# The expert sublayer of a two-layer decoder: sixteen more tokens take U's activations by fetched rows, the U tiles multiply 368 tokens instead of 384

## The chip, the core and the metric

The kernel runs on one core of a Trainium2 chip. A core has a matrix engine (TensorE, PE in the profile), a vector engine (VectorE, DVE), an activation engine (ScalarE, ACT), a general engine (GpSimd, POOL) and SyncE (SP), which here only issues transfers; 16 DMA engines move data between HBM and the on-chip memory SBUF. TensorE writes to a second memory, PSUM. Each engine runs its own list of instructions in order; they meet through semaphores. The metric is the device time of one execution in microseconds, as the median of several runs.

## The reference, cut to what matters

Each of two layers has a mixer and then an expert sublayer, which the change is about:

```python
def peer_ffn(h, w_query, sub_keys1, sub_keys2, expert_u, expert_v):
    """PEER: 8 retrieval heads over N = n_keys^2 single-neuron experts."""
    ...
    expert = e1 * PEER_NKEYS + e2           # 8 heads x 16 experts for each token, of 16384
    gate = softmax(top_v)
    act = gelu(einsum("td,thkd->thk", xt, expert_u[et]), approximate=False) * gt
    return einsum("thk,thkd->td", act, expert_v[et])
```

There are 512 tokens of width 1024, and 128 picked experts for each token. All data is float32.

## The kernel before

Matrices stream from HBM as tiles of 128x1024 (512 KB). The kernel splits each tile into a high part (`w_hi`, by ScalarE, line 729) and a low part (`w_lo`, by GpSimd at line 630 or by VectorE at line 2133), and a product is the sum of three: high by high, high by low, low by high. Ring buffers hold four tiles.

The experts are worked in two ways. For the first 384 tokens (`DENSE_T`) they are **dense**: the kernel computes the activations of all 16384 experts, and multiplies them by a matrix of gates that is zero where an expert isn't picked. For the last 128 tokens (one on each partition) they are **fetched**: for each of 128 picks GpSimd issues a gather of one row of U for each token (line 648), and VectorE multiplies it by the token's h and sums (line 2167, a "dot"; h lies in PSUM as `h_rows`, the name `gbank` in the rows); later the same with rows of V.

A layer's expert sublayer runs in this order, after the scores (8 heads, two halves):

- **U tiles**, 128 of them, `u_tile`: 8 blocks of 128 of the width, three products each, 24 matrix products with 384 moving columns in a tile (lines 1212 to 1214). ScalarE takes the gelu (line 973) and writes it to HBM.
- Beside U tiles 0 to 25 VectorE ranks the scores and ends with `ex`, the picked experts and their gates (line 2113). Then TensorE turns `ex` (line 1546, three groups of four), and ScalarE and VectorE make `exT`, `gate_lo` and the first one-hot planes from it.
- From U tile 26 on (`U_EARLY`), gates are made beside the U tiles: for every four tokens (a quad) VectorE makes one-hot planes (`hot` and `plane`, lines 2142 and 2147), ScalarE their low parts (line 1010), TensorE multiplies them in two pairs (line 1560), ScalarE takes the high half of the sums (line 1020) and VectorE adds the low half (line 2156). A pair comes every 49/12 eighths of a tile, so nearly two in a tile. TensorE's pair p waits for the sums of pair p-3 and for the planes of its quad.
- `turn_h`, before U tile 27: TensorE turns the 128 fetched tokens' h into `h_rows`, 16 products with 128 columns (line 1533). From there on GpSimd and VectorE work through U's fetched rows, nine in eight tiles (`rows_of`), with four buffers: the fetch of row j+3 waits for dot j-1. GpSimd's order in a tile is: the low part of the tile two ahead, then the fetches.
- **V tiles**, 128 of them, 18 products with 512 columns each (line 1232), beside them the last 15 dots of U and the 128 rows of V.

Neither the V tiles nor the mixers are touched by the change.

Of the kernel before, what the change touches and what calls it, by code (L numbers as in the profile page):

```python
# [5 lines left out]
F32 = mybir.dt.float32  # L6
# [32 lines left out]
DENSE_C = DENSE_T // P  # L39
PICKS = PH * TOPK  # L40
# [43 lines left out]
U_DOTS = max(rows_of(n).stop for n in range(U_EARLY, NKEYS))  # L84
# [45 lines left out]
def evacuators():  # L130
# [8 lines left out]
          "exT": 5, "hot": QUADS, "one": QUADS, "one_lo": QUADS, "gate_lo": 1, "g_mm": PAIRS_OF_TOKENS, "g_hi": PAIRS_OF_TOKENS, "g_out": PAIRS_OF_TOKENS, "stored0": 16 * PIECES * ((STORED + 1) // 2), "stored1": 16 * PIECES * (STORED // 2), "picked": 2,  # L139
          "h_rows": 1, "u_row": 16 * PICKS // U_ROWS, "v_row": 16 * PICKS // V_ROWS, "dotted": PICKS, "z_gel": 2,  # L140
# [81 lines left out]
def build(nc, stream, x_t, c, ada, ada_b, gains, gate_b, conv_w, mnorm, keys, qk_norm, u0, v0, u1, v1, out_t):  # L222
# [174 lines left out]
    u_rows = sb("u_rows", [P, U_ROWS, D])  # L397
    assert place[0] <= limit - 4 * DENSE_T * 4 - (limit % 64)
# [86 lines left out]
    def _(sp_):  # L485
# [75 lines left out]

        done = RING
        for layer in range(2):
# [10 lines left out]
            loads(done, DENSE[layer] + FIRST_UNIT_AT + UNIT_LEAD)  # L574
# [16 lines left out]
    def _(pool):  # L591
# [52 lines left out]
        def u_fetch(layer, j):  # L644

            past = counted(layer)
            wait(pool, S("dotted"), past["dotted"] + j - U_ROWS + 1)
            pool.indirect_dma_start(u_rows[:, j % U_ROWS, :], None, (u0, u1)[layer],  # L648
                                    bass.IndirectOffsetOnAxis(ap=row_of[:, j:j + 1], axis=0)
                                    ).then_inc(S(f"u_row{j % U_ROWS}"), 16)  # L650
# [9 lines left out]
        def peer(layer):  # L660

            past = counted(layer)
            for n in range(U_EARLY, U_GATED):
                if n == U_EARLY:
# [6 lines left out]
            for j in range(rows_of(U_GATED).start + U_ROWS - 1, min(PICKS, U_DOTS + U_ROWS - 1)):  # L671
                u_fetch(layer, j)
            pool.wait_ge(tile_done, DENSE[layer] + NKEYS)
            for j in range(PICKS):
                v_fetch(layer, j)
                dotted = dot_beside(j - V_ROWS)
                if dotted is not None and dotted + U_ROWS - 1 < PICKS:
                    u_fetch(layer, dotted + U_ROWS - 1)
# [42 lines left out]
    def _(act):  # L721
# [219 lines left out]
        def peer(layer):  # L941
# [23 lines left out]
            def u_tile(n, off=0, pairs=()):  # L965
# [7 lines left out]
                act.activation(gel[:, s, :], bank[t % 2][:, 0:DENSE_T], ACT.Gelu).then_inc(emptied_sem["a"], 1)  # L973
# [30 lines left out]
            def low_planes(q):  # L1004

                if q == 0:
                    act.wait_ge(S("gate_lo"), past["gate_lo"] + 1)
                act.wait_ge(S("hot"), past["hot"] + q + 1)
# [30 lines left out]
            for n in range(U_EARLY, NKEYS):  # L1039
# [1347 lines left out]
```

## Time and profile before

| | us |
|---|---|
| median of 3 runs | 3041.66 (3039.47 to 3042.04) |
| the profiled execution, its own time | 3040.28 |
| its span, first to last instruction | 3038.6 |
| TensorE busy | 2991.3 (98%) |
| VectorE busy | 2526.6 (83%) |
| GpSimd busy | 1589.9 (52%) |
| ScalarE busy | 1530.0 (50%) |
| moved by DMA | 846.18 MB, 278 GB/s on average |

The page's picture of the span in 40 slices shows where the stages lie: the U tiles of layer 0 run from 388 to 972 us and the V tiles to 1494 us; layer 1 has the same from 1921 and 2506 us. TensorE's busy digit is 9 in all slices but the first. The DMA digit is 4 to 6 in the tiles 0 to 25 of U, then 9. A share of busy time says little by itself: a matrix product's record is longer (0.33 us) than the distance to the next one, since they overlap. The pace is read from the distance of starts.

### The profile page before, as it was taken

Reading aid. Unit: us, or ns where it says so; the run is one execution under the profiler, and the core shown is the slowest. Engines: PE = TensorE matmul, PEld = TensorE weight load, DVE = VectorE, ACT = ScalarE, POOL = GpSimd, SP = SyncE. Lnnn points to the kernel's source line nnn. Section 1 sums busy time; section 2 is a strip of 40 time slices with the busy share of each in tenths; the row PEclk is TensorE's granted clock in tenths of the full one; section 3 lists DMA queues with packets and bytes.
Section 4 is the critical chain, followed back from the end, with each engine's and each line's share of the span. In section 5 each row is a group of like instructions: output and inputs, shape, how many; then the busy total and the mean of one; then the engine's idle time right before and its main releaser. Section 6 shows DMA issues by size and latency. Waiting matters only on the chain.

```text
span 3038.6 us, 45145 instructions
## 1 busy us (share of the span) xinstructions
PE 2991.3 (98%) x15480; PEld 2663.9 (88%) x15480; DVE 2526.6 (83%) x5006; ACT 1530.0 (50%) x2833; POOL 1589.9 (52%) x974
## 2 busy tenths in 40 slices
PE   6999999999999999999999999999999999999999
PEld 4888899999999888888787788999999998888887
DVE  7987998888887999998745949988888888888887
ACT  4345335776775333343464743347777763333332
POOL 3434357777776555452255634577777765322221
PEclk9999999999999999999999999999999999999999
DMA  6732246899999999999546422458999999999996
GB/s 256 248 110 104 85 156 220 323 325 345 344 325 360 395 391 393 390 391 373 190 164 211 115 66 84 140 196 310 333 326 355 334 357 374 384 373 366 346 351 229
DMA packets 320607, 846.18 MB, mean 278 GB/s; under 512 B 28208, under 2 KB 149056, under 8 KB 320400
## 3 DMA queue, kind: packets, MB, share of 16 engines
q1 hardware_dynamic: 189952, 437.83, 41.1%
q0 software_dynamic: 74000, 268.81, 24.0%
q10 hardware_dynamic: 56448, 136.86, 12.1%
q8 instruction: 119, 1.95, 0.3%
q14 instruction: 88, 0.72, 0.1%
HBM read 735.91 MB, written 94.90 MB: 273 GB/s over the span
## 4 chain that ended last, share of the span: by engine, by line
PE 90%; DVE 6%; ACT 2%; DMA 1%; issue 1%; ACTq 0%; DVEq 0%; SPq 0%; POOL 0%; POOLq 0%
PE banks L1232 23%; PE banks L1212 12%; PE banks L1214 12%; PE banks L1213 12%; PE gbank L1232 11%; PE banks L1192 4%; PE banks L1193 4%; PE banks L1194 4%; PE gbank L1560 2%; PE banks L1560 1%; PE gbank L1513 1%; PE banks L1291 1%; DMA ada_mid<-ada_dram 1%; DVE sp_lo L2311 1%; ACT sp L1115 1%
## 5 line engine op out<-in xcount | busy, mean ns | idle before, releaser
L630 POOL TENSOR_TENSOR w_lo<-raw,w_hi 128x1024 fp32r<-128x1024 f32 x351 | 901.9, 2573 | 537.4 <-ACT w_hi L729 534.4
L729 ACT ACTIVATE w_hi<-raw 128x1024 fp32r<-128x1024 f32 x613 | 646.5, 1055 | 601.0 <-PE banks L1232 373.4
L1212 PE MATMUL banks<-h_hi,w_hi 128*128 128x384 f32 x2048 | 687.0, 335 | 0.0
L1214 PE MATMUL banks<-h_hi,w_lo 128*128 128x384 f32 x2048 | 684.4, 334 | 0.0
L1213 PE MATMUL banks<-h_lo,w_hi 128*128 128x384 f32 x2048 | 684.3, 334 | 0.0
L656 POOL DMA_INDIRECT v_rows<-v_dram,row_of x256 | 356.1, 1391 | 619.6 <-DVE fetched L2182 603.6
L1212 PEld LDWEIGHTS banks<-h_hi,w_hi 128*128 128x128 f32 x2048 | 384.5, 188 | 0.0
L1213 PEld LDWEIGHTS banks<-h_lo,w_hi 128*128 128x128 f32 x2048 | 384.5, 188 | 0.0
L1214 PEld LDWEIGHTS banks<-h_hi,w_lo 128*128 128x128 f32 x2048 | 384.4, 188 | 0.0
L648 POOL DMA_INDIRECT u_rows<-u_dram,row_of x256 | 253.9, 992 | 204.9 <-DVE z L2167 169.9
L2182 DVE SCALAR_TENSOR_TENSOR fetched<-v_rows,share,fetched 128x1024 f32<-128x1024 f32 x254 | 326.5, 1285 | 3.6 <-DMA v_rows<-v_dram,row_of 3.2
L1232 PE MATMUL banks<-w_hi,a_hi 128*128 128x512 f32 x1024 | 315.3, 389 | 0.0
L1232 PE MATMUL banks<-w_lo,a_hi 128*128 128x512 f32 x1024 | 315.3, 389 | 0.0
L1232 PE MATMUL banks<-w_hi,a_lo 128*128 128x512 f32 x1024 | 315.3, 389 | 0.0
L2133 DVE TENSOR_TENSOR w_lo<-raw,w_hi 128x1024 fp32r<-128x1024 f32 x258 | 314.2, 1218 | 0.0
L2167 DVE CUSTOM_DVE_ANT_0 u_rows<-u_rows,gbank 128x1024 f32<-128x1024 f32 x256 | 308.9, 1214 | 0.0
L1010 ACT ACTIVATE plane<-hot,gate_lo 128x128 fp32r<-128x128 f32 x768 | 246.3, 391 | 83.6 <-ACT gel L973 66.6
L1192 PE MATMUL banks<-h_hi,w_hi 128*128 128x512 f32 x672 | 267.2, 398 | 2.2 <-POOL w_lo L630 2.2
L1194 PE MATMUL banks<-h_hi,w_lo 128*128 128x512 f32 x672 | 262.3, 390 | 0.0
L1193 PE MATMUL banks<-h_lo,w_hi 128*128 128x512 f32 x672 | 262.2, 390 | 0.0
L973 ACT ACTIVATE gel<-banks 128x384 f32<-128x384 f32 x256 | 125.7, 491 | 246.1 <-PE banks L1214 240.6
L2142 DVE TENSOR_TENSOR hot<-banks,exT 128x1024 fp32r<-128x1024 f32 x192 | 234.3, 1220 | 17.1 <-PE gbank L1560 10.5
(377 smaller groups left out, 5049.0 us busy)
## 6 DMA issues: line engine op xcount, KB each, us to landing
raw<-stream_dram SPq DMA_DIRECT2D x613, 512.0 KB, 6.5
gel_dram<-gel ACTq DMA_DIRECT2D x248, 192.0 KB, 4.2
gin<-gel_dram SPq DMA_DIRECT2D x62, 768.0 KB, 10.9
g_dram<-stage ACTq DMA_DIRECT2D x56, 768.0 KB, 9.4
gates<-g_dram SPq DMA_DIRECT2D x64, 672.0 KB, 7.3
ada_w<-ada_dram ACTq DMA_DIRECT2D x36, 512.0 KB, 7.4
ada_mid<-ada_dram ACTq DMA_DIRECT2D x24, 512.0 KB, 4.4
ada_first<-ada_dram SPq DMA_DIRECT2D x8, 1024.0 KB, 17.7
```

The costliest lines, as they stand in the source:

```text
L630: pool.tensor_tensor(w_lo[:, s, :], raw[:, s, :], w_hi[:, s, :].bitcast(F32), ALU.subtract).then_inc(split_lo, 1)
L656: pool.indirect_dma_start(v_rows[:, j % V_ROWS, :], None, (v0, v1)[layer], bass.IndirectOffsetOnAxis(ap=row_of[:, j:j + 1], axis=0)).then_ ...
L729: act.activation(w_hi[:, s, :], raw[:, s, :], ACT.Copy).then_inc(split_hi, 1)
L1192: pe.matmul(out, wh, hi(k), start=(k == 0), stop=False)
L1193: pe.matmul(out, wh, lo(k), start=False, stop=False)
L1194: mm = pe.matmul(out, wl, hi(k), start=False, stop=(k == DC - 1))
L1212: pe.matmul(out, wh, h_hi[:, k, 0:DENSE_T], start=(k == 0), stop=False)
L1213: pe.matmul(out, wh, h_lo[:, k, 0:DENSE_T], start=False, stop=False)
L1214: mm = pe.matmul(out, wl, h_hi[:, k, 0:DENSE_T], start=False, stop=(k == DC - 1))
L1232: mm = pe.matmul(sums[c][half][:], a, w[:, half * SEQ:(half + 1) * SEQ], start=(v == 0 and a is ah and w is hi), stop=(v == NKEYS - 1 and ...
L2133: dve.tensor_tensor(w_lo[:, s, :], raw[:, s, :], w_hi[:, s, :].bitcast(F32), ALU.subtract).then_inc(split_lo, 1)
L2182: add = dve.scalar_tensor_tensor(out=fetched[:], in0=row, scalar=share[:, j:j + 1], in1=fetched[:], op0=ALU.mult, op1=ALU.add)
```

## The change

In both layers, the last 16 of the 384 dense tokens no longer go through the U tiles: a U tile's products have 368 moving columns instead of 384. What those 16 tokens need is 16 x 128 = 2048 dots of a U row with their h. They are done as 16 more fetched rows in the same loop, rows 28 to 43 of now 144, an eighth of the picks of one token on each partition: partition 16 q + i holds the h of token i and, for the 16 rows, its picks 16 q to 16 q + 15. For that

- VectorE also computes the expert numbers of the last dense block (a memset and two small instructions after line 2123's place), and SyncE copies them and the gates, 16x16 pieces, to `row_extra` and `share_extra`: 16 small transfers, two ahead of each of 8 tile loads;
- TensorE turns the 16 tokens' h first (`turn_extra`, 16 products with a stationary block of 16 columns, before U tile 27), ScalarE copies it from PSUM to SBUF (`h_extra`, 16x1024), and SyncE copies it seven times down the partitions, one copy ahead of each of seven tile loads. `turn_h` is now before U tile 28 and waits for ScalarE's copy, since both use `h_rows`;
- the 16 extra dots read `h_extra`, which lies in SBUF, where the others read `h_rows` in PSUM;
- rows go at 23 in 18 tiles instead of 9 in 8, so that the V tiles have the same 15 dots as before;
- later ScalarE takes the gelu of the extra dots, VectorE multiplies by the gates and transposes blocks, SyncE gathers them back by 8 small transfers, and the result stands in the dense gates in the place of the 16 tokens' gates (`gate_extra_hi`, `gate_lo`). In the dense activations those tokens get the constant 1 (a copy of `ones` into `gel` once a layer), so V's products are as before;
- GpSimd takes the low part of tile 28 ahead of its first three fetches instead of behind them.

```diff
-    return range(min(PICKS, 9 * (n - ROWS_FROM) // 8), min(PICKS, 9 * (n - ROWS_FROM + 1) // 8))
+    return range(min(U_SUMS, 23 * (n - ROWS_FROM) // 18), min(U_SUMS, 23 * (n - ROWS_FROM + 1) // 18))
+U_SUMS = EXTRA + PICKS
+EXTRA_FROM = 28
...
+        def spread_extra(layer, q):
+            if q == 0:
+                sp_.wait_ge(S("picked"), counted(layer)["picked"] + 3)
...
+        def copy_extra(layer, q):
+            if q == 1:
+                sp_.wait_ge(S("extra_by_act"), counted(layer)["extra_by_act"] + H_ROWS_COPIED)
+            sp_.dma_start(h_extra[picks_of(q), :], h_extra[0:EXTRA, :]).then_inc(S("extra_moved"), 16)
...
             for n in range(U_EARLY, U_GATED):
+                low(DENSE[layer] + n + LOW_AHEAD)
                 if n == U_EARLY:
                     pool.wait_ge(S("picked"), past["picked"] + 2)
                     for j in range(U_ROWS - 1):
                         u_fetch(layer, j)
-                low(DENSE[layer] + n + LOW_AHEAD)
...
+                if n == ROWS_FROM:
+                    act.wait_ge(S("h_rows"), past["h_rows"] + 1)
+                    act.activation(h_extra[0:EXTRA, :], h_rows[0:EXTRA, :], ACT.Copy).then_inc(S("extra_by_act"), 1)
                 u_tile(n, pairs=[p for p in range(PAIRS_OF_TOKENS) if pair_step(p) // DC == n])
...
-                pe.matmul(out, wh, h_hi[:, k, 0:DENSE_T], start=(k == 0), stop=False)
-                pe.matmul(out, wh, h_lo[:, k, 0:DENSE_T], start=False, stop=False)
-                mm = pe.matmul(out, wl, h_hi[:, k, 0:DENSE_T], start=False, stop=(k == DC - 1))
+                pe.matmul(out, wh, h_hi[:, k, 0:DENSE_U], start=(k == 0), stop=False)
+                pe.matmul(out, wh, h_lo[:, k, 0:DENSE_U], start=False, stop=False)
+                mm = pe.matmul(out, wl, h_hi[:, k, 0:DENSE_U], start=False, stop=(k == DC - 1))
...
+            def turn_extra():
+                pe.wait_ge(S("exT"), past["exT"] + 2)
+                for k in range(DC):
+                    out = h_rows[0:EXTRA, k * P:(k + 1) * P]
+                    for n, h in enumerate((h_hi, h_lo)):
+                        last = pe.matmul(out, h[:, k, DENSE_U:DENSE_T], ident_r[:], start=(n == 0), stop=(n == 1))
+                last.then_inc(S("h_rows"), 1)
             def turn_h():
-                pe.wait_ge(S("exT"), past["exT"] + 2)
+                pe.wait_ge(S("extra_by_act"), past["extra_by_act"] + H_ROWS_COPIED)
...
                 if n == ROWS_FROM:
+                    turn_extra()
+                if n == ROWS_FROM + 1:
                     turn_h()
...
                 if j == 0:
-                    dve.wait_ge(S("h_rows"), past["h_rows"] + 1)
-                dve.tensor_tensor_reduce(row, row, h_rows, 1.0, 0.0, ALU.mult, ALU.add, z[:, j:j + 1]
-                                         ).then_inc(S("dotted"), 1)
+                    dve.wait_ge(S("h_rows"), past["h_rows"] + 2)
+                if j == EXTRA_FROM:
+                    dve.wait_ge(S("extra_moved"), past["extra_moved"] + EXTRA_COPIED)
+                e, m = j - EXTRA_FROM, main_row(j)
+                h, to = (h_extra[:], z_extra[:, e:e + 1]) if is_extra(j) else (h_rows, z[:, m:m + 1])
+                dve.tensor_tensor_reduce(row, row, h, 1.0, 0.0, ALU.mult, ALU.add, to).then_inc(S("dotted"), 1)
```

Two places show how the lists of instructions change. The first is ScalarE between `exT` and the gelu of U tile 27, in layer 0. In the kernel before (`plane` are the low one-hot planes of the first two quads, `w_hi` the high part of a tile three ahead, `gel` the gelu of tile 26):

```order
L1010 ACTIVATE plane<-hot,gate_lo 128x128 x8
L729 ACTIVATE w_hi<-raw 128x1024
L973 ACTIVATE gel<-banks 128x384
L976 DMA gel_dram<-gel 128x384
L729 ACTIVATE w_hi<-raw 128x1024
L1020 ACTIVATE stage<-banks 128x128x2
L973 ACTIVATE gel<-banks 128x384
```

In the changed kernel:

```order
L1098 ACTIVATE plane<-hot,gate_lo 128x128 x8
L812 ACTIVATE w_hi<-raw 128x1024
L1059 ACTIVATE gel<-banks 128x368
L1062 DMA gel_dram<-gel 128x384
L1130 ACTIVATE h_extra<-gbank 16x1024
L812 ACTIVATE w_hi<-raw 128x1024
L1108 ACTIVATE stage<-banks 128x128x2
L1059 ACTIVATE gel<-banks 128x368
```

The copy to `h_extra` stands behind the gelu of tile 26 and its store, and TensorE's `turn_h` waits for it.

The second is VectorE around U tile 49. In the kernel before (the pair `L2167 ISA` is one dot; its operand `gbank` is `h_rows` in PSUM):

```order
L2142 TENSOR_TENSOR hot<-banks,exT 128x1024
L2147 TENSOR_TENSOR plane<-hot,banks 128x4x128
L2156 TENSOR_TENSOR stage<-stage,gbank 128x128x2
L2167 ISA u_rows,z<-u_rows,gbank 128x1024
L2167 ISA z 128x1
```

In the changed kernel:

```order
L2257 TENSOR_TENSOR hot<-banks,exT 128x1024
L2262 TENSOR_TENSOR plane<-hot,banks 128x4x128
L2271 TENSOR_TENSOR stage<-stage,gbank 128x128x2 x2
L2286 ISA u_rows,z_extra<-u_rows,h_extra 128x1024
L2286 ISA z_extra 128x1
```

The dot's second operand is now in SBUF, as its first is, for 16 dots in a row; every other instruction of VectorE in this stage still reads one of its operands from PSUM.

## Rows read from the trace of the kernel before

**Rows 1.** The page: the chain that ended last, by engine.

```profile
PE 90%; DVE 6%; ACT 2%; DMA 1%; issue 1%; ACTq 0%; DVEq 0%; SPq 0%; POOL 0%; POOLq 0%
```

**Rows 2.** Timeline of TensorE, U tiles (start us, us, engine, line, names, shape).

```profile
440.29 0.33 PE L1212 MATMUL banks<-h_hi,w_hi 128*128 128x384 f32 x1
...
444.44 0.33 PE L1212 MATMUL banks<-h_hi,w_hi 128*128 128x384 f32 x1
```

**Rows 3.** The chain in order of time (start us, us, engine, line, count).

```profile
974.01 2.72 PE banks L1232 x12
978.09 2.72 PE banks L1232 x12
...
1809.49 2.88 PE gbank L1291 x24
```

**Rows 4.** Timelines of VectorE, then TensorE, before U tile 26 of layer 0.

```profile
493.41 1.67 DVE L2113 TENSOR_TENSOR ex<-ex,red 128x512 f32<-128x512 f32 x1
...
499.31 0.56 DVE L2125 TENSOR_TENSOR gate_lo<-gbank,hot 128x384 f32<-128x384 f32 x1 [3.51 <-ACT banks L1002]
...
495.93 1.47 PE L1546 MATMUL gbank<-ident,ex 128*128 128x128 f32 x12
```

**Rows 5.** Timeline of TensorE: turn_h, U tile 27, first pairs of tokens.

```profile
501.41 0.22 PE L1533 MATMUL gbank<-ident_r,h_hi 128*128 128x128 f32 x1
...
503.03 0.28 PE L1533 MATMUL gbank<-ident_r,h_lo 128*128 128x128 f32 x1
...
507.60 0.40 PE L1560 MATMUL gbank<-plane,hot 128*128 128x256 f32 x2
```

**Rows 6.** Timeline of ScalarE, the same stretch; then its splits of a tile (page).

```profile
505.64 0.34 ACTq L976 DMA_DIRECT2D gel_dram<-gel  x1
...
L729 ACT ACTIVATE w_hi<-raw 128x1024 fp32r<-128x1024 f32 x613 | 646.5, 1055 | 601.0 <-PE banks L1232 373.4
```

**Rows 7.** TensorE's waits (us in total, times, longest us).

```profile
PE banks L1270 <- ACT h_hi L790: 11.8, 2, 8.8
...
PE gbank L1600 <- ACT av L1104: 4.0, 2, 3.6
PE banks L1275 <- DVE h_lo L1801: 3.4, 2, 1.7
```

**Rows 8.** Stretches: busy time of the engines, TensorE's granted clock, DMA share, GB/s.

```profile
48.00:56.00 8.00, 5.59 (x23) 4.31 (x24) 5.39 (x10) 2.06 (x4) 0.00 (x0) 1.00 0.36 132
1508.80:1515.60 6.80, 5.82 (x14) 4.59 (x15) 6.80 (x12) 6.68 (x12) 0.00 (x0) 0.50 0.00 1
1655.55:1658.95 3.40, 3.40 (x14) 2.90 (x15) 2.52 (x5) 3.27 (x6) 2.99 (x2) 0.50 0.01 2
```

**Rows 9.** Line 1560, matrix products of a pair: idle time before it.

```profile
  issue: 3.5, 12
  DVE plane L2147: 1.2, 4
```

**Rows 10.** Stretches, as rows 8: 96 U tiles, then part of the V tiles.

```profile
515.00:960.00 445.00, 444.98 (x2675) 442.94 (x2673) 365.03 (x588) 318.09 (x754) 331.00 (x202) 1.00 0.93 336
1000.00:1400.00 400.00, 400.00 (x1767) 331.24 (x1766) 368.11 (x557) 150.97 (x199) 197.66 (x111) 1.00 1.04 391
```

**Rows 11.** Groups of instructions in 515 to 960 us (busy, mean ns, idle before).

```profile
L630 POOL TENSOR_TENSOR w_lo<-raw,w_hi 128x1024 fp32r<-128x1024 f32 x95 | 229.5, 2416 | 22.4 <-ACT w_hi L729 21.0
...
L2167 DVE CUSTOM_DVE_ANT_0 u_rows<-u_rows,gbank 128x1024 f32<-128x1024 f32 x108 | 130.2, 1214 | 0.0
```

**Rows 12.** VectorE's waits from 500 to 962 us, the longest.

```profile
DVE stage L2156 <- ACT stage L1020: 71.9, 94, 3.8
```

**Rows 13.** VectorE's groups, shapes apart, over the whole span.

```profile
L2133 DVE TENSOR_TENSOR w_lo<-raw,w_hi 128x1024 fp32r<-128x1024 f32 x258 | 314.2, 1218 | 0.0
...
L2106 DVE TENSOR_TENSOR pick<-pick 128x1024 f32<-128x1024 f32 x4 | 13.2, 3308 | 0.1
```

**Rows 14.** DMA issues in 515 to 960 us (count, median us to landing).

```profile
u_rows<-u_dram,row_of POOLq DMA_INDIRECT x107, 7.0
```

More of the change, by code:

```diff
@@ L39 @@
 DENSE_C = DENSE_T // P
+EXTRA = 16
+DENSE_U = DENSE_T - EXTRA
+GROUPS_OF_PICKS = P // EXTRA
+EXTRA_ROWS = slice(DENSE_U % P, DENSE_U % P + EXTRA)
 PICKS = PH * TOPK
@@ L397, in build @@
     u_rows = sb("u_rows", [P, U_ROWS, D])
+    h_extra = sb("h_extra", [P, D])
+    row_extra = sb("row_extra", [P, EXTRA], U32)
+    share_at = place[0]
+    share_extra = sb("share_extra", [P, EXTRA])
+    z_extra = sb("z_extra", [P, 2 * EXTRA])
+    gate_extra = z_extra[:, 0:EXTRA]
+    turned_extra = sb("turned_extra", [P, 2 * EXTRA])
+    u_end = place[0]
+    place[0] = share_at
+    gate_extra_hi = sb("gate_extra_hi", [P, EXTRA], F32R)
+    place[0] = u_end
     assert place[0] <= limit - 4 * DENSE_T * 4 - (limit % 64)
@@ L573, in _ @@
                 done = OUT1 + LEAD + RING
-            loads(done, DENSE[layer] + FIRST_UNIT_AT + UNIT_LEAD)
+            done_to = DENSE[layer] + U_EARLY + RING + 2
+            loads(done, done_to)
+            for q in range(GROUPS_OF_PICKS):
+                spread_extra(layer, q)
+                load_after(done_to + q)
+            done_to += GROUPS_OF_PICKS
+            for q in range(1, GROUPS_OF_PICKS):
+                copy_extra(layer, q)
+                load_after(done_to + q - 1)
+            loads(done_to + GROUPS_OF_PICKS - 1, DENSE[layer] + EXTRA_LOAD)
+            done_to = DENSE[layer] + EXTRA_LOAD
+            for q in range(GROUPS_OF_PICKS):
+                gather_extra(layer, q)
+                load_after(done_to + q)
+            loads(done_to + GROUPS_OF_PICKS, DENSE[layer] + FIRST_UNIT_AT + UNIT_LEAD)
             for s in range(2):
@@ L667, in peer @@
                         u_fetch(layer, j)
-                low(DENSE[layer] + n + LOW_AHEAD)
                 for j in rows_of(n):
                     u_fetch(layer, j + U_ROWS - 1)
-            for j in range(rows_of(U_GATED).start + U_ROWS - 1, min(PICKS, U_DOTS + U_ROWS - 1)):
+            for j in range(rows_of(U_GATED).start + U_ROWS - 1, min(U_SUMS, EXTRA + U_DOTS + U_ROWS - 1)):
                 u_fetch(layer, j)
@@ L677, in peer @@
                 if dotted is not None and dotted + U_ROWS - 1 < PICKS:
-                    u_fetch(layer, dotted + U_ROWS - 1)
+                    u_fetch(layer, EXTRA + dotted + U_ROWS - 1)
         lows(RING, DENSE0 + U_EARLY + LOW_AHEAD)
@@ L1053, in gelu_rows @@
                 own = slice(n * Z_HALF, Z_HALF if n == 0 else PICKS)
[L1054 removed]
+                act.wait_ge(S("dotted"), past["dotted"] + EXTRA + own.stop)
                 act.activation(z[:, own], z[:, own], ACT.Gelu).then_inc(S("z_gel"), 1)
@@ L1205, in u_tile @@
             pe.wait_ge(emptied_sem["a"], emptied("a", t - 2) + off)
-            out = bank[t % 2][:, 0:DENSE_T]
+            out = bank[t % 2][:, 0:DENSE_U]
             for k in range(DC):
@@ L2123, in peer @@
             dve.tensor_copy(share[:], last_ex[2]).then_inc(S("picked"), 1)
+            extra_ex = [ex[:, n, DENSE_C - 1].rearrange("p h k -> p (h k)") for n in range(2)]
+            dve.memset(z_extra[:, EXTRA:], 0.0)
+            link(dve.scalar_tensor_tensor(out=z[:], in0=extra_ex[0], scalar=float(NKEYS), in1=extra_ex[1],
+                                          op0=ALU.mult, op1=ALU.add))
+            dve.tensor_copy(expert[:].bitcast(U32), z[:]).then_inc(S("picked"), 1)
             dve.wait_ge(S("exT"), past["exT"] + 5)
@@ L2231, in peer @@
                 if dot_beside(v) is not None:
-                    dot(dot_beside(v))
+                    dot(EXTRA + dot_beside(v))
                 add_row(v)
```

64 lines of the change are left out of this document (57 added, 7 removed).

## The prediction

> **What bounds the kernel now.** I read the chain that ended last first: nine tenths of it are TensorE [rows 1], so time goes where TensorE's own list gets shorter, and stays where the next engine is late. Then the pace of its products, from the distance of starts. In the U tiles 24 products take 444.44 - 440.29 = 4.15 us, 173 ns each, for 384 columns [rows 2]. A V tile's 18 products of 512 columns come every 4.08 us, 227 ns each, and 24 products of 256 columns take 2.88 us, 120 ns each [rows 3]. The three lie on one line: 0.417 ns for a column, and 13 ns beside. So columns are the bound in the U tiles, and 16 fewer are worth 16 x 0.417 = 6.7 ns a product. That weight loads set the pace, so that narrower products win nothing, is excluded by the 120 ns.
>
> Then, for each engine that hands something to TensorE, how late it already is: before tile 26 [rows 4], at tile 27 [rows 5, 6], at the pairs [rows 9], and over the 96 tiles beside the gates [rows 10 to 12].
>
> **What the columns bring.** 24 x 6.7 ns = 0.16 us a tile, 128 tiles, two layers: -41.0 us.
>
> **Where the first part of it goes: tile 26.** TensorE starts to turn `ex` at 495.93 [rows 4], 12 products at 0.11 us (1.47 us less the overlap of the last); the last four start at 496.8. They need the last `ex`, which VectorE ends at 493.41 + 1.67 = 495.08 [rows 4], only 1.7 us earlier. VectorE isn't held by TensorE there, so its time stays, while TensorE comes 26 x 0.16 = 4.16 us earlier, at 492.65. It waits until about 495.2: 2.55 us lost in a layer, +5.1 us for both. VectorE's own additions behind that (a memset of 16 columns, a sum and a cast of 128) are each shorter than the 0.56 us of 384 columns behind them, which sits idle for 3.51 us on ScalarE [rows 4]; of that cover 1.6 goes with the earlier turns and 1.9 is left for under 1.7, so they are hidden. GpSimd's low part of tile 28 moves 2.4 us of work [rows 11] ahead of three fetches; these land late by as much, but the first dot now waits longer anyway, for `turn_h`.
>
> **Tile 27 and 28.** `turn_extra` is 16 more products of 128 columns. The same count in `turn_h` takes 503.03 - 501.41 and one more, 1.75 us [rows 5]; a stationary block of 16 columns instead of 128 may be quicker to load, and 128 columns can't pass in less than 53 ns each: 0.9 to 1.8 us; I take 1.1. Then `turn_h` waits for the copy to `h_extra`. ScalarE issues tile 26's store at 505.64 for 0.34 us [rows 6]; its work there hangs on `exT`, so it comes 1.6 us earlier, and ends at 504.4. The copy has 1024 columns, as a split of a tile, 1.06 us [rows 6]: done at 505.5. TensorE: tile 26 from 495.55, 4.0 us, turn_extra 1.1, tile 27 with a pair 4.24: there at 504.9, waits 0.65, then `turn_h`. With 1.8 instead of 1.1 it comes when the copy is done, so either value gives the same. Cost 1.75 us a layer, +3.5. After this the pair that now starts at 507.60 [rows 5] starts at 507.4: of the first 28 tiles' 4.5 us, 0.2 is left.
>
> **The clock.** A wait of 2.55 us is new. The longest waits in this trace are 3.6 us and (11.8 less 8.8) 3.0 us [rows 7], and behind each the granted clock is 0.50 (1.2 GHz) for 3.4 and 6.8 us [rows 8]; two waits of 1.7 us [rows 7] lie in a stretch at 1.00 (2.4 GHz) [rows 8]. Mine lies between. 3.4 us at half rate cost 1.7 us, of which 0.65 would have been waited for the copy: 1.05 a layer. Bounds: none, or 6.8 us twice, 5.5 us. I take one fall in one of the two layers, +1.0.
>
> **The pairs.** TensorE stood idle before a pair 16 times, 4.7 us in all [rows 9]: where an odd pair opens a tile, the next pair needs planes that ScalarE starts only behind the gelu. There the half tile before gets no shorter: 16 x 0.08 = +1.3.
>
> **VectorE and the shared way.** VectorE is busy 365.03 of 445 us, 3.81 of 4.64 us a tile [rows 10] (the 4.64: 24 products of 173 ns, and 1.96 pairs of two products at 120 ns); 23/18 rows instead of 9/8 add 0.153 x 1.214 us [rows 11], so 4.0 of 4.48. Its idle time is mostly a wait for ScalarE, 71.9 us [rows 12], which a late VectorE doesn't have. But the 16 extra dots have both operands in SBUF. Such an instruction and GpSimd's low part shut each other out here: an addition of 1024 columns takes 3308 ns where GpSimd splits, a subtraction of the same shape 1218 ns where it doesn't [rows 13], against 2416 ns for an undisturbed low part [rows 11], so about one low part is waited for. The Trainium skill has this as a rule (SBUF — State Buffer, "Who interferes with whom"): a VectorE instruction with two SBUF inputs contends with a GpSimd instruction that reads SBUF, and the later one waits for the whole of the other. It speaks against this change, and the trace agrees, by the rows just named. GpSimd is at a low part for 2.42 of 4.48 us. A dot can wait 0 to 2.42 us, so 0 to 38.7 us a layer. If a dot waited for a low part, the next one is due just when the next low part starts or ends, so VectorE settles a fixed 1 to 2 us behind and TensorE, which needs the sums only three pairs later, about 7 us, sees little. I take 0.5 us a layer, +1.0.
>
> **Rows that land late.** A fetched row lands 7.0 us after its issue (median) [rows 14]. Four rows pass between a buffer's turns: 4 x 4.64 / 1.125 = 16.5 us now, 4 x 4.48 / 1.278 = 14.0 then, less dot, issue and a low part, about 4.6: 9.4 us. The 16 rows are 8.4 MB more, and the rate goes from 336 GB/s to some 365, under the 391 of the V tiles [rows 10]. In bursts some rows will be late. 0 to 2 us a layer, taken as 0.5, +1.0. SyncE's small transfers stand between tile loads and take nothing that TensorE sees; the two waits on it are for things long done when the loads ahead have been let go.
>
> **Sum.** -41.0 + 5.1 + 3.5 + 1.3 + 1.0 + 1.0 + 1.0 = -28.1. Against the profiled execution's 3040.28: 3012.2. The median of the runs is 1.4 above that: 3013.6.
>
> **Rivals.**
>
> *Dots queue behind low parts, and it shows* (no change): each extra dot waits half a low part, 1.2 us. 16 x 1.2 = 19.4 us a layer; the 12.5 tiles they lie in have 0.48 us to spare each, 6 us, so 13.4 is left, 26.8 in both, instead of the 1.0 above: 3039.4. For it: the rows on the lock. Against: the slack of three pairs, and that waits for ScalarE vanish when VectorE is late. Cases between this and the forecast are likelier than the full one.
>
> *The same lock, and slower than before*: each extra dot waits for a whole low part, 2.42 us: 38.7 - 6 = 32.7 a layer, 65.4 in both: 3078. From 1.3 us of wait a dot on, all slack used, the change loses. For it: in the first tiles beside gates the low part starts just ahead of the dot, tile after tile. Against: VectorE, once late, starts behind the low part.
>
> *The DMA engines are the bound*: their share is 0.93 in this stretch [rows 10]. If 336 GB/s were all that this mix can carry, 8.4 MB would take 25 us in a layer, and the stage grows by that instead of shrinking by 16: 3041.66 + 50 = 3092. Against: 391 GB/s a little later, and that VectorE's list has no wait for a row among its longest.
>
> **How the numbers follow.** The forecast, 3008 to 3019: 0.6. Between it and the first rival, 3019 to 3035: 0.26. The first rival in full, 3035 to 3048: 0.06. Slower, by the lock 0.05, by the DMA engines 0.03. The lower end has none of clock, lock and late rows: 3010.6, and some for error in the pace: 3008. The upper end adds the bounds 4.5 (clock), 8 (lock, half seen) and 2 (rows): 3028. A measurement of this kernel can tell 0.2%, 6 us, from no change: faster 0.86, same 0.06, slower 0.08.
>
> **What would show it.** U tiles 4.0 us apart before tile 26 (right: the pace). TensorE waiting some 2.5 us on VectorE at the turns of `ex`, about 0.65 us on ScalarE before `turn_h`. V tiles of layer 0 starting 14 to 15 us earlier than 972. Extra dots of up to 3.6 us in VectorE's rows with the low parts beside them (the lock); TensorE's waits on line 2156's sums or on low parts in the tiles 49 to 61 would say that it shows. Wrong it would be if U tiles stay at 4.16 us, if the dots wait for rows tile after tile, or if VectorE's ranking itself moves with the faster tiles.

## The result, and the profile after

The changed kernel takes 3017.55 us in the median (3015.15 to 3018.09, 4 runs) against 3041.5 before (3039.47 to 3042.04, 4 runs): a ratio of 0.9921, with a 95% interval of 0.9906 to 0.9937. It is 24 us faster. The forecast was 3013.6, 28 us faster, and the range 3008 to 3028. The profiled execution took 3017.35 us, its span is 3015.6.

The pace first. TensorE's timeline among the early U tiles (start us, us, engine, line, operation; line 1309 is line 1212 of before). Eight products of this line, so 24 in all, are one tile:

```profile
447.81 0.33 PE L1309 MATMUL banks<-h_hi,w_hi 128*128 128x368 f32 x1
...
451.81 0.33 PE L1309 MATMUL banks<-h_hi,w_hi 128*128 128x368 f32 x1
```

4.00 us a tile against 4.15 in [rows 2]. Next the place of [rows 4], TensorE's first product of U and the turns of `ex`:

```profile
388.21 0.41 PE L1309 MATMUL banks<-h_hi,w_hi 128*128 128x368 f32 x1
...
492.31 1.47 PE L1652 MATMUL gbank<-ident,ex 128*128 128x128 f32 x12
```

and VectorE's last step of the ranking (line 2221 for 2113) and its subtraction for `gate_lo`, which has no idle time ahead of it any more:

```profile
490.74 1.68 DVE L2221 TENSOR_TENSOR ex<-ex,red 128x512 f32<-128x512 f32 x1
...
495.69 0.56 DVE L2238 TENSOR_TENSOR gate_lo<-gbank,hot 128x384 f32<-128x384 f32 x1
```

The ranking ends at 492.42, 104.2 us behind U's first product. Before it was 495.08 - 387.65 = 107.4. The last four of the turns' products, which need it, start at 493.18: of the 1.7 us that it was ahead of them, 0.8 is left, though TensorE came earlier, and the wait that I had put at 2.55 us does not exist. Then the turn of the 16 rows, and ScalarE's copy of them, the places of [rows 5, 6]:

```profile
497.64 0.22 PE L1630 MATMUL gbank<-ident_r,h_hi 128*16 128x128 f32 x1
...
498.53 0.22 PE L1630 MATMUL gbank<-ident_r,h_lo 128*16 128x128 f32 x1
```

```profile
502.40 1.01 ACT L1130 ACTIVATE h_extra<-gbank 16x1024 f32<-16x1024 f32 x1 [0.42 <-ACT gel L1059]
```

Sixteen products come 0.06 us apart, and tile 27 starts at 498.59: about 1.0 us. What TensorE waits for in the whole span, as in [rows 7] (us in total, times, longest):

```profile
PE banks L1367 <- ACT h_hi L873: 11.8, 2, 8.8
...
PE gbank L1666 <- DVE stage L2271: 6.2, 2, 3.1
PE gbank L1708 <- ACT av L1201: 4.5, 2, 3.7
...
PE gbank L1329 <- DVE w_lo L2246: 1.3, 3, 0.7
...
PE gbank L1639 <- ACT h_extra L1130: 0.8, 2, 0.4
```

The wait for the copy is there, 0.4 us in each layer. The largest new row is another: 3.1 us, twice, for line 2271, VectorE's addition to `stage`, ahead of a pair of tokens. It stands at the very end of U, in both layers. TensorE's timeline there, and two stretches with the clock (columns as [rows 8]):

```profile
941.88 0.32 PE L1311 MATMUL banks<-h_hi,w_lo 128*128 128x368 f32 x1
945.29 0.47 PE L1666 MATMUL gbank<-plane,hot 128*128 128x256 f32 x2 [3.09 <-DVE stage L2271]
```

```profile
942.00:946.00 4.00, 0.91 (x7) 0.74 (x6) 1.28 (x3) 2.17 (x5) 1.51 (x1) 1.00 1.02 409
946.04:949.45 3.41, 3.41 (x13) 3.41 (x12) 2.85 (x7) 2.69 (x5) 1.91 (x3) 0.50 0.75 262
```

VectorE had waited for ScalarE, and ScalarE (first row below, its waits from 880 to 950 us) for a tile of the stream, 7.1 us. The chain that ended last goes through that tile's transfer (second row). Behind the wait the granted clock is 0.50 for 3.41 us: 13 products pass instead of 20, 1.7 us more.

```profile
ACT w_hi L812 <- DMA raw<-stream_dram: 7.5, 2, 7.1
```

```profile
924.17 19.17 DMA raw<-stream_dram
```

That transfer stands on SyncE's queue behind the loads of V's first two units. The DMA issues of 515 to 960 us (KB each, median us to landing) show them slower than in the kernel before, where the same three rows were 5.9, 11.3 and 16.3; below, the stretches of [rows 10]:

```profile
raw<-stream_dram SPq DMA_DIRECT2D x98, 512.0 KB, 6.6
...
gates<-g_dram SPq DMA_DIRECT2D x2, 672.0 KB, 14.2
gin<-gel_dram SPq DMA_DIRECT2D x1, 768.0 KB, 19.5
```

```profile
515.00:940.00 425.00, 424.00 (x2636) 421.22 (x2635) 383.12 (x611) 307.52 (x744) 350.09 (x214) 1.00 0.97 361
1000.00:1400.00 400.00, 398.66 (x1755) 328.81 (x1754) 364.33 (x553) 152.07 (x200) 209.69 (x110) 1.00 1.03 386
```

361 GB/s are the some 365 of the working, with a share of 0.97. Last, the dots (VectorE's groups, whole span, shapes apart) and a wait that the kernel before does not have, VectorE's for rows from 500 to 962 us:

```profile
L2286 DVE CUSTOM_DVE_ANT_0 u_rows<-u_rows,gbank 128x1024 f32<-128x1024 f32 x256 | 307.4, 1213 | 14.6 <-DMA u_rows<-u_dram,row_of 13.3 <-PE gbank L1639 1.0
L2286 DVE CUSTOM_DVE_ANT_0 u_rows<-u_rows,h_extra 128x1024 f32<-128x1024 f32 x32 | 52.1, 1642 | 0.8 <-DMA u_rows<-u_dram,row_extra 0.8
```

```profile
DVE u_rows L2286 <- DMA u_rows<-u_dram,row_of: 6.0, 5, 3.1
```

Where the 23.0 us between the two profiled spans lie, from the starts of the tiles in both traces (U counted from its first product to V's first): U got shorter by 12.4 us in layer 0 and 12.2 in layer 1; V is longer by 2.5 us in layer 0 and as long in layer 1 (522.1); the parts between and around are 0.9 us shorter.

### The profile page after: what moved, and what is told of

The parts are those of the page before. It is cut to its first block, busy times and chain, and to the rows that moved or that the text cites. A ratio compares the mean times of both kernels' runs of the same rounds, so it can differ in the third digit from the quotient of the medians.

```text
span 3015.6 us, 45245 instructions
## 1 busy us (share of the span) xinstructions
PE 2957.6 (98%) x15512; PEld 2624.1 (87%) x15512; DVE 2571.4 (85%) x5084; ACT 1521.9 (50%) x2841; POOL 1680.1 (56%) x1006
## 4 chain that ended last, share of the span: by engine, by line
PE 56%; DVE 23%; DMA 11%; issue 4%; ACT 4%; POOL 1%; SPq 0%; ACTq 0%; DVEq 0%; POOLq 0%
PE banks L1329 16%; PE gbank L1329 8%; DMA raw<-stream_dram 8%; PE banks L1309 6%; PE banks L1310 6%; PE banks L1311 6%; PE banks L1289 3%; PE banks L1291 3%; PE banks L1290 3%; DVE u_rows L2286 2%; DVE hot L2257 2%; DVE pick L2214 2%; DVE w_lo L2246 1%; PE gbank L1666 1%; DVE pick L2209 1%
## 5 line engine op out<-in xcount | busy, mean ns | idle before, releaser
L739 POOL DMA_INDIRECT v_rows<-v_dram,row_of x256 | 392.0, 1531 | 576.0 <-DVE fetched L2300 561.7
L1309 PE MATMUL banks<-h_hi,w_hi 128*128 128x368 f32 x2048 | 676.4, 330 | 0.0
L1310 PE MATMUL banks<-h_lo,w_hi 128*128 128x368 f32 x2048 | 674.0, 329 | 0.0
L1311 PE MATMUL banks<-h_hi,w_lo 128*128 128x368 f32 x2048 | 673.9, 329 | 0.0
L1329 PEld LDWEIGHTS banks<-w_lo,a_hi 128*128 128x128 f32 x1024 | 192.2, 188 | 40.0
```

The source lines that it names most:

```text
L739: pool.indirect_dma_start(v_rows[:, j % V_ROWS, :], None, (v0, v1)[layer], bass.IndirectOffsetOnAxis(ap=row_of[:, j:j + 1], axis=0)).then_ ...
L1309: pe.matmul(out, wh, h_hi[:, k, 0:DENSE_U], start=(k == 0), stop=False)
L1310: pe.matmul(out, wh, h_lo[:, k, 0:DENSE_U], start=False, stop=False)
L1311: mm = pe.matmul(out, wl, h_hi[:, k, 0:DENSE_U], start=False, stop=(k == DC - 1))
L1329: mm = pe.matmul(sums[c][half][:], a, w[:, half * SEQ:(half + 1) * SEQ], start=(v == 0 and a is ah and w is hi), stop=(v == NKEYS - 1 and ...
```

## The experiments

Each is set against runs of the kernel before on the same chip. Their median was 3040.5 us beside most of them, against 3041.5 beside the changed kernel, so medians of two batches can differ by 1 us for nothing. A trace is of one run: with full width it is the slowest of seven, with the dots, the early turn and both moves the fastest of four.

**The second unit's loads behind the stream.** The edit in SyncE's program:

```
-            for u in range(2):
-                load_unit(layer, u)
+            load_unit(layer, 0)
             for t in range(DENSE[layer] + FIRST_UNIT_AT + UNIT_LEAD, v0_ + NKEYS):
+                if t == v0_:
+                    load_unit(layer, 1)
```

> The changed kernel with one move on SyncE's queue: the loads of the second unit of V (its gates) are issued behind the last two raw tiles of the stream instead of ahead of them; the first unit's loads stay where they are. In the changed kernel TensorE stands for 3.1 us twice before the last tiles of U (in each layer; ScalarE had waited 7.1 us for a stream tile then) and the granted clock is 0.50 for 3.41 us behind it; I put this at about 4.8 us per layer. Theory (the last stream tiles of U land late because the units' loads are ahead of them in the queue): the waits of ScalarE and of TensorE at tiles 124 and 125 go, the clock stays at 1.00 there, and the time falls by 6 to 10 us, to about 3009. Rival (the DMA engines are full there whatever the order): the 3.1 us remain or only move to V's first tile, and the time is within 2 us of the changed kernel, 3016 to 3019.

The second unit's loads are `gates` and `gin`, 1.44 of the 2.1 MB that stood ahead of those tiles.

Measured: 3008.52 us (3006.08 to 3012.17), ratio 0.9901, 0.9884 to 0.9918. The stretch that was at a stand, and TensorE's waits from 480 to 950 us:

```profile
942.00:946.00 4.00, 4.00 (x26) 4.00 (x25) 2.83 (x6) 0.89 (x2) 2.41 (x3) 1.00 1.05 410
```

```profile
PE banks L1667 <- DVE stage L2272: 1.1, 1, 1.1
PE banks L1310 <- POOL w_lo L710: 0.5, 1, 0.5
PE gbank L1640 <- ACT h_extra L1131: 0.4, 1, 0.4
```

26 products where there were 7, at the same 410 GB/s, no stand and no fall of the clock in either layer. U is 3.2 and 5.0 us shorter than in the changed kernel; 1.4 us of layer 0's part went again at tile 61, behind a low part of GpSimd that came late (the 0.5 above), and at tile 82, where VectorE had waited 2.5 us for a late row (the 1.1). So the order on the queue makes the wait, and not only the full DMA engines. The time fell by 9 us against the changed kernel by the medians, which come from two batches; the two intervals of the ratio overlap, so the size rests on the traces, the mechanism on the row that went.

**The columns alone.** The kernel before with one constant changed in three products and the gelu. It leaves out the activations of the last 16 dense tokens, and copies a constant into their place once a layer:

```
-                pe.matmul(out, wh, h_hi[:, k, 0:DENSE_T], start=(k == 0), stop=False)
+                pe.matmul(out, wh, h_hi[:, k, 0:DENSE_U], start=(k == 0), stop=False)
```

> The kernel before with U's products and the Gelu 368 columns wide, and nothing else of the change: the activations of the last 16 dense tokens are left out (a constant stands in their place), no rows are added for them, nothing is copied or turned for them. It shows the columns alone. The early tiles should take 4.00 us against 4.16. What it tells apart. (a) The end of U: if the faster tiles alone make the stream late there, TensorE waits about 3 us at tiles 124 and 125 in this kernel too, and the time is about 3013; if it takes the added rows as well, the wait is not there and the time is about 3003 (3017.5 less 3.5 for the turns and their wait, less about 1 for the late rows, less 9.6 for the end of U). (b) The ranking: my prediction held that its end stands at 107.4 us from the first tile of U, so that tile 26 waits for some 2.5 us per layer; the rival that the changed kernel suggests is that this end moves by some us with the phase in which VectorE's and GpSimd's steps meet (it stood at 104.2 us there). If the end stands at 107.4 here, the tiles' pace does not move it and the changed code behind it did; if it stands at 103 to 106, the phase does.

Measured: 3000.12 us (2998.77 to 3000.35), ratio 0.9869, 0.9852 to 0.9885: 40.4 us less, of the sum's 41.0, and 3 below the lower of my two figures. V's tiles start 20.1 us earlier behind U's start in both layers. At the end of U ScalarE waits up to 2.3 us for a tile of the stream, but TensorE doesn't stand, so the faster tiles alone do not make its wait. And the ranking, with not one instruction of it changed, ends at 489.63 + 1.68 = 491.31, 104.2 us behind U's first product, as in the changed kernel. Answer to (b): the change's code did not move it, the pace did. What it ends with is a low part of GpSimd (second row, which ends at 490.76, 0.55 us ahead; third row, the same place in the kernel before, which ends 0.55 us ahead of 495.08):

```profile
489.63 1.68 DVE L2118 TENSOR_TENSOR ex<-ex,red 128x512 f32<-128x512 f32 x1
487.89 2.87 POOL L632 TENSOR_TENSOR w_lo<-raw,w_hi 128x1024 fp32r<-128x1024 f32 x1
491.67 2.86 POOL L630 TENSOR_TENSOR w_lo<-raw,w_hi 128x1024 fp32r<-128x1024 f32 x1
```

**All additions at the old width.** The reverse: the changed kernel with `DENSE_T` in those products.

> The changed kernel with U's products as wide as before, 384 columns (the last 16 dense tokens are then computed twice, the fetched way still gives the result): all that the change adds, without what it takes away. By the prediction's sums the additions on TensorE's path are 3.5 us for the turns and the wait for the copy, 1.3 at the pair waits and 1 for the late rows, 5.8 in all, so 3046 or so against 3040.3 of the kernel before. Theory (the end of U waits because the faster tiles meet an almost full DMA): at 4.16 and 4.64 us per tile the wait at tiles 124 and 125 is gone or under 1 us, and the time is 3044 to 3048. Rival (the denser rows alone make the stream late): the 3.1 us and the clock's fall remain, and the time is 3052 to 3056. If the extra dots cost more than they seem to (their lock on GpSimd's low parts), this shows too: each further 0.1 us per tile of the late stage is 18 us.

Measured: 3047.96 us (3043.76 to 3051.77, 7 runs), ratio 1.0025, 1.0014 to 1.0037. The additions cost 7.5 us at the old width and some 17 at the new one (3017.55 less 3000.12, of two batches). In the profiled execution (3051.77, the slowest) the turns cost 1.4 us a layer and the late rows nothing up to tile 124. The end of U is between the two expectations: TensorE waits there in both layers, 1.1 and 2.7 us, and the clock falls behind the longer one.

```profile
PE gbank L1666 <- DVE stage L2271: 3.7, 2, 2.7
```

So in these traces the narrow tiles alone make no wait, the added rows alone 3.7 us, and both 6.2. The ranking ends at 107.4 us here, though the changed code is all there.

**Dots without the second operand in SBUF.**

```
-                h, to = (h_extra[:], z_extra[:, e:e + 1]) if is_extra(j) ...
+                h, to = (h_rows, z_extra[:, e:e + 1]) if is_extra(j) ...
```

> The changed kernel with the added dots reading the common rows of h in PSUM, as the others do, instead of the copy of the 16 tokens' rows in SBUF: the U activations of the last 16 dense tokens are then made with other tokens' h and are wrong, everything else is as it is. Without two operands in SBUF the added dots should no longer hold each other up with GpSimd: in the changed kernel they take 1.85 us in the median (1.21 the least), and GpSimd's fetches with added rows 1.76 (0.95 the least). Theory (that wait is hidden: TensorE is never late by it): the added dots take 1.21, the fetches 0.95, and the time stays within 3 us of the changed kernel, 3015 to 3019, since the end of U waits for the stream as before. Rival (my prediction's: the lock costs TensorE 0.26 to 0.54 us per tile over the late stage): 3017.5 less 8 or more, under 3010.

Measured: 3015.49 us (3012.99 to 3018.66), ratio 0.9922, 0.9905 to 0.9938. The dots and GpSimd's fetches from 600 to 655 us (ns min, median, max), first of the changed kernel, then of this one:

```profile
L2286 DVE CUSTOM_DVE_ANT_0 u_rows<-u_rows,h_extra x14: 1215/1849/2100, 606.0 to 654.1; 128x1024 f32<-128x1024 f32 x14
L731 POOL DMA_INDIRECT u_rows<-u_dram,row_extra x14: 932/1757/1821, 602.7 to 653.2; - x14
```

```profile
L2286 DVE CUSTOM_DVE_ANT_0 u_rows<-u_rows,gbank x16: 1212/1214/1217, 601.0 to 652.4; 128x1024 f32<-128x1024 f32 x16
L731 POOL DMA_INDIRECT u_rows<-u_dram,row_extra x14: 934/950/952, 602.5 to 649.0; - x14
```

The lock is real and goes with the operand: 0.64 us on a dot, 0.81 on a fetch. Who waits for whom is seen in the changed kernel's timelines (VectorE, then GpSimd):

```profile
613.79 2.10 DVE L2286 CUSTOM_DVE_ANT_0 u_rows<-u_rows,h_extra 128x1024 f32<-128x1024 f32 x1
612.37 2.42 POOL L709 TENSOR_TENSOR w_lo<-raw,w_hi 128x1024 fp32r<-128x1024 f32 x1
614.95 1.76 POOL L731 DMA_INDIRECT u_rows<-u_dram,row_extra  x1 [0.16 <-issue]
```

The dot starts inside a low part and ends 1.1 us behind the low part's end (614.79); it waited for the low part's rest, and the fetch, issued behind the low part, for the dot. The dots of 1.21 us that meet a fetch already under way are not held.

The edit bought no time that the runs can tell. By the traces TensorE is 1.1 to 1.4 us further at tile 124 than in the changed kernel, so late rows and lock together cost about 2.5 us, both layers summed; the small losses at tiles 61 to 82 are gone. This kernel's V stage in layer 0 is 4.0 us longer than before, against 2.5.

**The 16 rows' turn one step earlier.** `turn_extra` ahead of U tile 24, the copy behind the gelu of that tile, `turn_h` back ahead of tile 27 (PE shown; ScalarE's copy moves with it):

```
+            turn_extra()
             for n in range(4 + (U_EARLY - 4) // 4 * 4, U_EARLY):
                 u_tile(t0 + n)
+            pe.wait_ge(S("extra_by_act"), past["extra_by_act"] + H_ROWS_COPIED)
...
                 if n == ROWS_FROM:
-                    turn_extra()
-                if n == ROWS_FROM + 1:
                     turn_h()
```

> The changed kernel with the turn of the 16 tokens' rows one step earlier: it stands ahead of U tile 24, ScalarE copies the rows behind its Gelu of tile 24, and the common turn of h stands where it did in the kernel before, ahead of tile 27, with the same wait for the ranking. In the changed kernel TensorE stands about 0.7 us in each layer behind the turn, waiting for ScalarE's copy, whose Gelu and stage come first. Theory: this wait goes, ScalarE's copy of 1.01 us costs nothing on TensorE's path, and 1.4 us are saved in both layers, 3016.1; the end of U then waits as before or some tenths longer, since the stream is no earlier: 3016 to 3017.5. Rival (ScalarE is late by its copy in that stage, and the tile behind waits for its emptied bank or for its w_hi): the 0.7 us come back at tiles 25 to 27, no gain or a loss of up to 2 us.

Measured: 3018.83 us (3013.4 to 3021.8), ratio 0.9935, 0.9918 to 0.9952: no gain. Up to tile 28 it did what it should: the wait for the copy is gone and, from U's first product, TensorE is 0.7 us earlier than in the changed kernel in both layers (0.69; the 0.85 of the next expectation is too high). In layer 1 the end of U took it back, as the row of TensorE's wait there shows (6.2 before this edit); in layer 0 it was gone before, with 1.6 us lost at tiles 60 and 61, where a low part of GpSimd came late behind a fetch that had waited for a dot:

```profile
PE gbank L1668 <- DVE stage L2271: 8.4, 2, 5.1
```

**Both moves.** 

> The changed kernel with both moves: the 16 tokens' turn and ScalarE's copy one step earlier, and the second unit's loads behind the last stream tiles. Alone, the second gave 3008.5 with no wait at the end of U; the first gave 0.85 us per layer ahead of tile 28, and lost it again at the end of U, where the waits grew to 3.3 and 5.1 us. Theory (what the early turn saves is given back only because the stream is late there): with the stream early the 0.85 us stay in both layers, 3008.5 less 1.7, 3006.8 (3004 to 3009). Rival (the early turn costs at tiles 60 to 62, where the run of it alone lost 1.3 us in the first layer): 3008 to 3010.

Measured: 3009.92 us (3003.23 to 3010.57), ratio 0.9901, 0.9884 to 0.9917. The profiled run is the fastest, 3003.23, with its 0.7 us kept up to tile 28 in both layers and no stand at the end of U; the other three are not faster than the loads' order alone. The early turn is therefore not shown to bring anything. Nor did I find out why these runs lie in two places, 7 us apart.

**Other widths: 376, 352, 356 and 372.** The first three are the columns-alone kernel with another constant, with one run each; the last is the changed kernel with the later loads and four columns more in U's products.

> The kernel before with U's products 376 columns wide (the activations of the last 8 dense tokens left out, a constant in their place), a tile of 4.08 us instead of 4.16. The ranking of the routes has no idle time and the same instructions at every width; its end stands at 107.4 us from the first tile of U at 384 columns and at 104.2 at 368, the same to 0.03 us in both layers and in kernels with and without the added rows. Theory (the phase of VectorE's steps against GpSimd's decides, and every step outside of the meetings has the same length): the end here is anywhere from 102 to 109 us and need not lie between the two. Rival (a faster pace makes the ranking end sooner, in proportion): 105.8, and 101 at 352 columns. The time should be 3040.5 less 0.08 x 256, 3020, within 3.

> As the run at 376 columns, with U's products 352 columns wide (the activations of the last 32 dense tokens left out), a tile of 3.84 us. Phase theory: the ranking's end stands anywhere from 102 to 109 us from U's first tile; it then comes about 0 to 7 us behind tile 26, which stands at 101.2, and tile 26 waits as my prediction had it for the changed kernel. Rival (in proportion to the pace): 101, and no wait. Time by the columns alone 3040.5 less 82, 2958.5; with the wait in both layers up to 10 more, and more if the stream's DMA or ScalarE becomes the bound at this pace.

> The kernel before with U's products 356 columns wide (the activations of the last 28 dense tokens left out, a constant in their place). At 384, 376, 368 and 352 columns a U tile of 24 products took 4.16, 4.16, 4.00 and 3.84 us: the 376 cost what 384 do. Theory (a product's time goes in steps of 16 columns): 356 cost what 368 do, 4.00 us per tile, the ranking's end stands at 104.2 us, and the time is about that of the run at 368 columns, 3000. Rivals: steps of 8 columns from a multiple of 32 (360: 3.92 us per tile, 2984 or so); time by the column, with 376 a special case (3.87 us per tile, 2973 or so, with up to 6 us of waits for the ranking).

> The changed kernel with the second unit's loads behind the last stream tiles, as in the run that gave 3008.5, and U's products 372 columns wide instead of 368 (four of the 16 tokens are then computed in the dense way too; the fetched way still gives the result). Early U tiles of 24 products took 4.16 us at 384 and at 376 columns, 4.00 at 368, and 3.84 at 356 and (late in the stage, 3.87 early) at 352: 173.3, 166.7 and 160.0 ns a product, at the clock of 2.4 GHz 416, 400 and 384 cycles. All five fit one rule: the columns and 25 to 28 cycles beside them, rounded up to a multiple of 16 cycles. By this rule 372 columns cost 400 cycles: 4.00 us per tile, and the time is that of the run with 368, 3008.5, within 3 us. Rival (the steps lie at multiples of 16 columns, with 356 a special case): 4.16 us per tile, and 0.16 x 256 = 41 us more, near 3045. The time also measures the gain by the loads' order a second time.

Measured: 3039.88, 2967.0, 2962.55, and 3024.3 (3022.82 to 3027.54; ratio 0.9947, 0.993 to 0.9963). How many products TensorE has in the same 80 us of early U tiles: 464 at 384 columns, 482 at 368, and at 376, 372, 356 and 352 columns, one row each (stretch, its length, busy time and count, clock, DMA share, GB/s):

```profile
400.00:480.00 80.00, 80.00 (x464) 1.00 0.54 173
```

```profile
400.00:480.00 80.00, 80.00 (x473) 1.00 0.52 175
```

```profile
400.00:480.00 80.00, 80.00 (x502) 1.00 0.54 180
```

```profile
400.00:480.00 80.00, 80.00 (x499) 1.00 0.55 179
```

By the tiles' starts, for 384, 376, 372, 368, 356 and 352, that is 173.3, 173.3, 170.0, 166.7, 160.0 and 161.1 ns a product. Eight columns less than 384 brought nothing at all; 356 cost less than 352 in these early tiles, and the same in the later ones (520 products from 600 to 680 us in both). My expectation of 3020 for 376 was wrong, as was each rule that I wrote down for the next run: the steps of 16 columns fell with 356, the rounding to 16 cycles with 372, where neither it nor its rival came out. I have no rule for these times. The forecast's straight line through 256, 384 and 512 columns held for 368 because 368 happens to lie on it: at 376 it gives 170.0, and 173.3 was measured.

The last run measured the loads' order again, in another way: at 4.08 us a tile, no wait at the end of U in either layer.

**The ranking, moved by hand.** The kernel before, with one step that no one waits for done three times, or six:

```
+            for _ in range(2):
+                link(dve.memset(fifteen[:], TOPK - 1))
             dve.memset(fifteen[:], TOPK - 1)
```

> The kernel before, all 384 columns, with one step of VectorE's ranking done three times (the fill of the tile fifteen, 0.485 us, which no one waits for), so that all later steps of the ranking meet GpSimd's low parts about 1.0 us later than they do; tiles, stream and GpSimd stay as they are. So far the ranking's end stood at 107.4 us from U's first tile at 4.16 us per tile, at 104.2 at 4.00 and at 102.3 at 3.84: by tile pace or by phase. Phase theory (the long adds of the ranking are held for as long as a low part of GpSimd overlaps them, and the overlap moves when the steps move): the end moves by something other than the 1.0 us put in, anywhere from -3 to +4 us. Rival (the length of the ranking is set by the pace alone): the end at 108.4, to 0.3 us. The time stays within 3 us of the kernel before, since the turns behind tile 26 wait for the ranking's end only if it stands beyond tile 26's end at 109.5.

> As the run with the step done three times, with six: about 2.6 us put in ahead of the ranking's second half. Phase theory: the end is not at 107.4 + 2.6, and the two runs' moves are not in the proportion 1.0 to 2.6. Rival (pace alone): the end at 110.0, and U tile 26 waits 0.5 us for it in both layers, one us in all.

Measured: 3038.85 and 3041.93 us, one run each, beside 3039.51. The ranking's end stands at 107.4 us (three times) and at 109.75 (six times), from U's first product. So 1.3 us of work put in (the two extra fills and their waits, more than the 1.0 that I had expected) moved the end by nothing. The place where it went, timeline of VectorE and GpSimd, first of the kernel before (U's first product at 387.65), then of the three fills (387.83):

```profile
432.39 2.38 DVE L2092 CAST i16f<-i 128x1024 f32<-128x1024 uint32 x1
431.82 2.40 POOL L630 TENSOR_TENSOR w_lo<-raw,w_hi 128x1024 fp32r<-128x1024 f32 x1 [1.71 <-ACT w_hi L729]
```

```profile
432.88 0.48 DVE L2092 MEMSET fifteen<- 128x512 uint32 x1 [0.17 <-DVE fifteen L2091]
433.86 1.07 DVE L2094 CAST i16f<-i 128x1024 f32<-128x1024 uint32 x1
431.98 2.40 POOL L630 TENSOR_TENSOR w_lo<-raw,w_hi 128x1024 fp32r<-128x1024 f32 x1 [1.71 <-ACT w_hi L729]
```

The cast of 1024 columns takes 2.38 us, starts 44.74 us behind U's start and ends at 47.12 before; with the fills it starts at 46.03, takes 1.07 and ends at 47.10. Both times it ends 0.55 us behind the end of the same low part. VectorE was held there until GpSimd let go, and what was put in ahead of it only filled the hold. With six fills (3.3 us put in) the cast comes behind that low part and takes 0.68, the ranking's last step meets none and takes 0.69 instead of 1.67, and the end moved by 2.3. In every other kernel here that last step ends 0.55 us behind a low part's end. TensorE then waited 0.5 us for it in each layer, as expected.

## Why the prediction was right, and where not

The time lay in the range, 4 us above the forecast, and faster was right. By its own steps, both layers together, in us:

- **Columns**, -41.0: the columns alone measured -40.4, the loss at the pairs within it. Right here, by luck in its reasoning, as the widths show.
- **The wait for `ex`**, +5.1: measured 0. This step failed: "VectorE isn't held by TensorE there, so its time stays". VectorE has no idle row in the ranking, but its steps there are not free-running: those that meet a low part end with it, and low parts follow the tiles. The ends behind U's first product are 107.4 us at 4.16 us a tile (at 376 columns too), 105.7 at 4.08, 104.2 at 4.00, 102.3 at 3.87 and 102.0 at 3.84, the same within 0.1 us in both layers. At 3.87 and 3.84 the ranking no longer keeps up, and TensorE waits 0.7 and 1.1 us for `ex`. The prediction named this as a way to be wrong ("if VectorE's ranking itself moves with the faster tiles"), and it is what happened.
- **Turn and copy**, +3.5: 1.0 us for the products and 0.4 counted as a wait; with what stands between, TensorE is 1.7 us a layer behind the columns-alone kernel at tile 28, 3.4. Right.
- **The clock at tile 26**, +1.0: no wait, so no fall. Measured 0. Its size came true elsewhere: behind the 3.1 us waits at the end of U, 3.41 us at 0.50 each, in both layers.
- **The pairs**, +1.3: about 1.0. The eight tiles in a layer that held such waits shrank by some 0.10 instead of 0.16. Right.
- **Lock, and late rows**, +1.0 each: together about 2.5. The Trainium skill's rule on two SBUF inputs (SBUF — State Buffer, "Who interferes with whom"), that the later one waits until the other is through, agrees with the trace: only the dots with both operands in SBUF are long, and they end 1.1 us behind the low part that they met. In size they waited 0.64 us in the median, and none more than 0.9, since those that waited came in the second half of their low part; at its start it would have been up to 2.42. Both rivals on the lock are out by this, as is the DMA rival: 361 GB/s passed at a share of 0.97, and up to 410 in short stretches.
- **Not in the sum: the end of U**, +9.7. I had read the waits of 500 to 962 us as a whole and the landing of rows, but not the slack of the last stream tiles, whose loads stand behind 2.1 MB of the first units on SyncE's queue. In the kernel before ScalarE waits 0.6 us for a stream tile there: the stream had no lead. The rate was in the working, the order of the loads on the queue was not, and moving one unit's loads removed both waits.
- **Not in the sum: V of layer 0**, +2.5, four short waits of TensorE. Every kernel with the added rows has 0.5 to 4.0 us of it, except the one at 4.08 us a tile with the later loads (0.03). Of the kernels without them the one at 376 columns has 1.5, the others none, so the added rows are not needed for it. Its cause stays open.

So that the forecast was near is in part luck: 6.1 us of cost that did not come stood against 12.2 that I had not seen. The rest differs by -0.9 between and around the stages.

## What to carry to other kernels

Before a stretch gets faster, read the slack of every transfer that is queued behind a burst at the stretch's end, not the mean share of the engines; here the order of two loads was worth about as much as all other costs of the change together. An engine without idle time can still be paced by another: if its steps come in two lengths, put some work in ahead and see whether the end moves. And time the width that you will use, since the matrix products here don't get cheaper column by column.

## What the hardware did that I had not expected

- The same product of early U tiles took 173.3 ns at 384 and at 376 columns, 170.0 at 372, 166.7 at 368, 160.0 at 356 and 161.1 at 352.
- 1.3 us of added work on a busy VectorE cost nothing, since a cast behind it was held by GpSimd's low part and shrank from 2.38 to 1.07 us.
- GpSimd's fetch instruction went from 0.95 to 1.76 us beside VectorE's dots with two operands in SBUF. The hold goes both ways: dots wait for low parts, fetches for dots.
- At the end of U TensorE's waits of 2.7 to 5.1 us were followed by 3.41 us at a granted clock of 0.50 (1.2 GHz) in six of seven cases. The seventh wait, 3.0 us in layer 0 with the dots from PSUM, left the clock at 1.00, though the same wait in layer 1 did not; the waits of 1.1 to 1.4 us there left it at 1.00 too.
